# Starting the four folds of the samples' sums later and spacing them closer, with a shorter lead before each add

## The reference, cut to what matters

```python
def block(xb):                       # peer_ffn: tokens by D = 1024
    ...                              # scores, top-16 per head -> eidx, gate
    u = u_tab[eidx]
    a = jax.nn.gelu(jnp.einsum('pd,ped->pe', xb, u))
    coef = gate.astype(xb.dtype) * a
    return jnp.einsum('pe,ped->pd', coef, v_tab[eidx])
...
f = peer_ffn(h, w_q, sub_keys, u_tab, v_tab)
x = x + gt2[:, None, :] * rms_norm(f, g_post2)
```

## Time and profile before

| | |
|---|---|
| median of 3 runs | 1856.24 us (1853.55 to 1856.55) |
| the profiled execution | 1853.55 us, span 1851.7 us |
| mean granted clock of TensorE | 0.982 |
| PE busy over the span | 1769.9 us, 96% |
| DVE busy | 1087.3 us, 59% |
| ACT busy | 584.0 us, 32% |
| POOL busy | 1037.7 us, 56% |
| bytes moved by DMA | 383.61 MB, 207 GB/s on average |

### The profile page before, as it was taken

One profiled execution on the slowest core, in us unless ns is written; L12 is line 12 of the kernel. 1 busy time (PEld: TensorE's weight loads), 2 busy tenths in 40 slices (PEclk: granted clock), 3 DMA queues, 4 the chain that ended last, 5 costly groups with the idle time before them and its releaser, 6 DMA issues.

```text
span 1851.7 us, 31249 instructions
## 1 busy us (share of the span) xinstructions
PE 1769.9 (96%) x12760; PEld 1710.6 (92%) x12760; DVE 1087.3 (59%) x2181; ACT 584.0 (32%) x753; POOL 1037.7 (56%) x684
## 2 busy tenths in 40 slices
PE   5799998899999999999999999999999999999996
PEld 4799975778999999999999999999999999999995
DVE  4731464545747746666664222222788889888884
ACT  5313151333323332233232222222333333333332
POOL 0240010000577778888888888773776777767630
PEclk9899997899999999999999999999999999999998
DMA  7332275766346666575666766666999999999971
GB/s 270 128 146 78 95 290 204 228 202 223 88 87 129 140 129 138 104 155 121 138 124 133 150 138 138 138 138 206 350 374 364 379 366 373 358 372 373 373 299 47
DMA packets 191399, 383.61 MB, mean 207 GB/s; under 512 B 74192, under 2 KB 131920, under 8 KB 176280
## 3 DMA queue, kind: packets, MB, share of 16 engines
q1 hardware_dynamic: 111576, 307.08, 49.3%
q0 software_dynamic: 79680, 74.53, 18.5%
HBM read 316.86 MB, written 64.18 MB: 206 GB/s over the span
## 4 chain that ended last, share of the span: by engine, by line
PE 56%; DVE 9%; issue 5%; DMA 1%; ACT 0%; DVEq 0%; SPq 0%; ACTq 0%
PE ps L1474 29%; PE ps L1454 27%; DVE ul L1644 2%; DVE topi L134 1%; DVE topi L124 1%; DMA ahead_dram<-a 1%; DVE top L128 1%; PE ps L1431 0%; DVE h L227 0%; DVE h L222 0%; DVE h L213 0%; DVE pick L217 0%; DVE pick L234 0%; DVE h L206 0%; ACT uh L1511 0%
## 5 line engine op out<-in xcount | busy, mean ns | idle before, releaser
L99 POOL DMA_INDIRECT gates_dram<-gate,where x384 | 642.6, 1674 | 331.1 <-DVE where L250 187.1
L1454 PE MATMUL ps<-hl,uh 128*128 128x260 f32 x2048 | 414.2, 283 | 8.8 <-DVE ul L1644 8.8
L1454 PE MATMUL ps<-hh,ul 128*128 128x260 f32 x2048 | 413.9, 284 | 0.0
L1454 PE MATMUL ps<-hh,uh 128*128 128x260 f32 x2048 | 413.3, 283 | 0.0
L1644 DVE TENSOR_TENSOR ul<-us,uh 128x1024 fp32r<-128x1024 f32 x132 | 161.2, 1224 | 363.8 <-issue 276.0
L1474 PE MATMUL ps<-cl,uh 128*128 128x384 f32 (+1 forms) x1024 | 344.7, 337 | 0.7 <-issue 0.7
L1474 PE MATMUL ps<-ch,uh 128*128 128x384 f32 x1024 | 344.1, 336 | 0.0
L1474 PE MATMUL ps<-ch,ul 128*128 128x384 f32 x1024 | 344.1, 336 | 0.0
L1454 PEld LDWEIGHTS ps<-hl,uh 128*128 128x128 f32 x2048 | 316.9, 189 | 9.9 <-DVE ul L1644 9.7
L1454 PEld LDWEIGHTS ps<-hh,ul 128*128 128x128 f32 x2048 | 316.9, 189 | 0.0
L1454 PEld LDWEIGHTS ps<-hh,uh 128*128 128x128 f32 x2048 | 316.1, 189 | 0.0
(11 more groups left out here) (212 smaller groups left out, 2233.8 us busy)
## 6 DMA issues: line engine op xcount, KB each, us to landing
us<-utab SPq DMA_DIRECT2D x128, 512.0 KB
pairs<-vtab SPq DMA_DIRECT2D x62, 1024.0 KB
wr<-w_ada SPq DMA_DIRECT2D x24, 1024.0 KB, 6.2
gates_dram<-blank SPq DMA_DIRECT2D x24, 1024.0 KB, 8.6
ahead_dram<-a SPq DMA_DIRECT2D x128, 192.0 KB
qp<-ahead_dram SPq DMA_DIRECT2D x32, 768.0 KB
gt<-gates_dram SPq DMA_DIRECT2D x32, 768.0 KB
wr<-w_in SPq DMA_DIRECT2D x14, 1024.0 KB, 4.8
```

The source lines that it names most:

```text
L99: nc.gpsimd.indirect_dma_start(out=io["gates"].rearrange("g p c a t -> (g p c a t)").unsqueeze(1), out_offset=bass.IndirectOffsetOnAxis(ap ...
L1454: last = nc.tensor.matmul(out[:, half, :], w, r[:, k, half * TH:(half + 1) * TH], start=(k == 0 and q == 0), stop=(k == KD - 1 and q == 2))
```

## The change

The first copy moves from step 24 to step 30, the spacing from 10 steps to 4, and the add from 7 steps behind its copy to `FOLD_EVERY // 2` = 2 steps behind it. `SAMPLES_AT`, which is derived, moves from 64 to 46, and with it the root on ACT and `sample_norm`. No instruction and no transfer is added or taken out.

| | SP's copies | DVE's adds | sample_sums | root | sample_norm |
|---|---|---|---|---|---|
| before, steps | 24, 34, 44, 54 | 31, 41, 51, 61 | 64 | 66 | 68 |
| after, steps | 30, 34, 38, 42 | 32, 36, 40, 44 | 46 | 48 | 50 |

```diff
@@ -1215,7 +1215,7 @@
     PACK_AT, PACKED_AT = 84, 88
     FOLDS = (64, 32, 16, 8)
-    FOLD_AT, FOLD_EVERY, FOLD_LAG = 24, 10, 7
+    FOLD_AT, FOLD_EVERY = 30, 4
     SAMPLES_AT = FOLD_AT + FOLD_EVERY * len(FOLDS)
@@ -1744,7 +1744,7 @@
                     while n >= 0 and sums[0] < summed(n):
                         gathered()
-                    fold_n, at = divmod(n - FOLD_AT - FOLD_LAG, FOLD_EVERY)
+                    fold_n, at = divmod(n - FOLD_AT - FOLD_EVERY // 2, FOLD_EVERY)
                     if at == 0 and 0 <= fold_n < len(FOLDS):
                         fold(fold_n)
```

## The result

The changed kernel takes 1867.56 us (median of 5 runs, 1863.71 to 1873.51), the kernel before 1856.24 (5 runs, 1853.35 to 1857.68). The ratio is 1.0059 [1.0036, 1.0084]: slower by 0.59%, some 11.0 us (0.0059 x 1856). The ratio is formed from the undisturbed executions and need not be the quotient of two medians. I predicted 4.75 us and a time of 1861.0, at most 1866.5. The sign was right. The size was not: the loss is more than twice the sum, and the time lies 1.1 us above the range.

What follows compares the result with a forecast made beforehand. PE was taken to bound the second loop. Its waits of 0.2 + 0.5 + 2.05 + 1.15 + 0.85 sum to 4.75 us, added to the median 1856.24 for 1861.0 us, range 1855.5 to 1866.5.

Steps and rivals of the forecast that it cites:

- The work fits: Steps 32 to 50: DVE's moved work, 8.0 us plus double gathers 4.2 and small products 0.6, against 16.9 us recoverable.
- The account of DVE's lateness: Second loop: DVE's lateness per step falls 0.89 us, grows by added work; PE waits for any excess over 4.4 us.
- L: Time from a fold copy's issue to its landing: between 7.2 and 11.2 us, taken as 10.3, with 0.6 more for fold 0.
- with 10.9 the first adds 2.65: Fold 0, issued at step 30: a copy landing after 10.9 us adds 2.65 us to DVE's lateness.
- D(33): DVE's lateness at the start of step 33, behind fold 0's add: 3.45 us, with no loss of PE.
- what waits behind DVE's stalled add: Claimed `ul`, `cl` and next coefficients, hence PE; SP's loads up to 4 us late but with lead; POOL's gather merely following its buffer.
- 4.4 us of lead: Second loop at rest: DVE has `ul` ready 4.4 us early, so PE waits only when DVE is later than that.
- L1694 where they didn't: Sign in DVE's gather waits: new waits there would mean the queue is slower under the new order than assumed.
- The clock: PE's waits in the loop, up to 2.05 us, counted as causing no lower clock; one such stretch would add about 1.7 us.
- the longer loss: Rival, chance 0.13: bursts in full queues hold a copy or gather longer; landing after 12 us loses 11.5 us, 1866 to 1870.
- The copies in time: Rival, chance 0.32: copies land in under about 9 us, DVE never exceeds its lead, time 1856.2 to 1858 us.
- The faster kernel: Rival, chance 0.03: steps 51 to 68 lose 5.75 us of DVE's work; time 1856.2 us or immeasurably under it.

Runs made afterwards that it cites:

- the gap: DVE waits in every loop step for its own coefficient product (L1673) to end; on the changed kernel 1861.79 us, on the kernel before 1855.47 us.
- experiments 8: The changed kernel with the add 3 steps behind its copy instead of 2, and the gap in every step: 1856.22 us, 1.0002.
- experiment 10: The changed kernel with the gap, and SP issuing the copy ahead of the loads `aa` and `gt` of the same step: 1854.74 us, 0.9988.
- experiment 5: The changed kernel with the gap in every step, copies still issued by SP behind the loads: 1861.79 us, 1.0034 against the kernel before.
- experiment 2: The changed kernel with the add 3 steps behind its copy instead of 2, without the gap: 1865.3 us, 1.0035 against the kernel before.
- experiment 4: The changed kernel with SP copying only 64 of the 1024 columns, without the gap: 1864.12 us, 1.0059 against the kernel before.
- experiment 12: The kernel before with one more 400-element DVE add in steps 20 to 119, and the gap in every step: 1873.09 us, 1.0089.

## Why the prediction was half right

**The bound, the place and the sign were right.** PE bounds the loop; PE's waits in it all stand at L1474, behind `ul`. `sample_sums` costs PE 0.53 us (predicted 0.85). The work fits, as I had added it up: with copies in time and the gap, the 19 steps lose nothing (experiments 8 and 10, both with a loop of 536.8 us).

**The account of DVE's lateness was right for fold 0, its L was not.** The term "with 10.9 the first adds 2.65" was mis-sized: L was 14.0 us in the changed kernel, 12.5 in experiment 5 (1431.82 - 1419.27). With 14.0 the account gives D(33) = 0.8 + 14.0 - 8.25 = 6.55, thus a wait of PE of 2.15 us; measured 2.41. With the 12.5 of experiment 5 it gives 0.7; measured 1.00. These are its only sharp tests. The trace before had the number: its copy of fold 0 passed its last packet 13.5 us after the issue. I had read 9 to 10 us from the mean packet size of one stretch, where half of its rows were through and not the last. For the others I took 10.3; before, their last packets ended after 9.8, 9.7 and 8.0 us, so the value was fair there. In experiment 5 the adds of folds 1 and 2 began 10.2 and 8.8 us after the issue. In the changed kernel fold 2's add took 9.2, and folds 1 and 3 were through after 5.5 and 7.0 us. So L was too short for fold 0 and too long for the rest. I predicted waits at the adds of 1.8, 3.4, 3.6 and 2.0 us, and the changed kernel had 4.95, 0, 1.64 and 0. Why the copies take so long is only in part known. For fold 1 a sixteenth of the bytes changes nothing (10.5 us), so what stands ahead matters; in ACT's queue, with nothing ahead, the last packets came 1.3 to 3.7 us sooner, but fold 0's still after 8.0; ahead of the loads they came 1 us sooner at most (experiment 10). The place in the queue is thus part of it and not all. The 2.0 us plus bytes of the Trainium skill, "DMA: Bandwidth & Descriptors", Anatomy of one DMA, gave an estimate of 2.6 us for the copy. This case's trace doesn't agree with that as a time under load: even alone in ACT's queue fold 0's add began 9.2 to 9.4 us after the issue.

**The step that failed** is the last part of "what waits behind DVE's stalled add": "and POOL's next gather, which only follows the use of its buffer". I costed the gathers at nothing. They do follow the use of their buffer, but the time that their issue takes also depends on DVE's pauses. At rest DVE pauses 0.8 us in each step. A late DVE skips that pause. I had put this down as pure gain (0.89 us won back a step), and it is just this state in which an issue can take 4 to 15.5 us. Then DVE runs out of gathers: it waited 3.98 us in the changed kernel, and up to 7.80 in experiment 2. With what it was late already, that is more than its 4.4 us of lead. That is the wait "L1694 where they didn't", which I had named as a sign of a slower queue; the transfers weren't slower, the issues were. The kernel before already holds two, 4.09 us at 1428.38 and 5.70 at 1505.37, the second as a fold's add ended, the first 5 us behind one. At the second, DVE is late behind the add of fold 2 and skips its next pauses, and POOL's issue beside it lasts until 1511.07, 0.8 us after the next pause began (1510.75 - 0.51 = 1510.24):

```profile
1504.10 1.27 DVE L1701 TENSOR_TENSOR fg<-fg,keys 16x1024 f32<-16x1024 f32 x1
...
1510.75 0.56 DVE L1678 TENSOR_TENSOR cl<-qp,ch 128x384 fp32r<-128x384 f32 x1 [0.51 <-ACT ch L1540]
```

```profile
1505.37 5.70 POOL L1608 DMA_INDIRECT qp<-vtab,packed_choice  x1 [0.30 <-issue]
```

There a single add made DVE late, it was back at its pauses after two steps, and the 4.4 us covered the rest.

**How much is whose.** Removing the held issues alone takes the loss from 11.0 to 6.3 us. Making the copies punctual alone leaves +6.5 with a third step, where no add waits. With small copies (+10.9) and in ACT's queue (+12.8) one or two adds still waited, up to 2.4 us. With the gap as well these are +0.4, +1.7 and +1.1 us. With the third step the two savings, 4.7 and 4.5 us, nearly add up to the 10.6 of both, within their intervals; with the other two they don't, since sooner copies alone saved nothing. That a late copy takes away DVE's pauses, and a held gather makes DVE later still, would explain this; it is argued. With held gathers gone, 6.3 us remain (4.5 to 8.2 by its interval), for late copies. The profiled execution of that kernel is 8.0 us longer than before: 2.8 of them ahead of the loop, 0.8 behind it, where the kernels do not differ, and 4.5 in the loop. That is close to the 4.75 predicted for late copies alone, but in part by luck, for it does not lie where it was predicted. PE's matmuls waited 1.00 us behind fold 0 (predicted: nothing), 0.95 and 0.35 behind fold 1 (0.7), 0.37 behind fold 2 (2.05), nothing behind fold 3 (1.15) and 0.36 behind `sample_sums` (0.85).

**The clock.** "My waits are up to 2.05 us, so I count none, but one such stretch would add about 1.7 us": the stretch came, at the end of a wait of 2.41 us, and cost about that. In the loops of all profiled executions every wait of PE of 2.56 us or more has such a stretch beside it, none of 1.65 us or less has, and of the four between, 2.41 (twice), 2.34 and 2.23, one of 2.41 hasn't (experiment 4). The stretch of experiment 2, at its wait of 5.77 us:

```profile
1478.50:1485.30 6.80, 4.76 (x15) 4.76 (x16) 6.80 (x9) 1.47 (x2) 5.47 (x5) 0.50 0.76 260
```

**The rivals.** Of the longer loss I had the outcome (1866 to 1870; 1867.56 came) and named a held gather in passing, from the 2.57 us in the earlier trace rows, but priced it by L = 12, hence as a transfer held in its queue. It got 0.13. The row that should have raised it was in the trace: the issue of 5.70 us at 1505.37, among 136 with a median of 1.3, in the very loop and just behind a fold's add, with that wait of 2.57 at 1519.24 after it. The copies in time fell with fold 0's 14.0 us. The faster kernel did not come: the 5.75 us of work taken from steps 51 to 68 bought nothing, as PE was never short there.

## What to carry over

An engine that stands idle for a moment in each step may be giving another engine its only chance to get work out: before counting that pause as slack that can be used up, look at the longest, not the median, duration of what the neighbour issues. Where long issues show up, try a deliberate short wait in the busy engine's step; here under 0.1 us of pause in each step was worth 5 to 12 us. It cost nothing in the kernel before, and gained nothing where DVE's work was itself near the bound (experiment 12). And a DMA's lead is read from the last of its packets in a trace of the loaded kernel, not from the mean of its packets: for the 256 KB of fold 0 the last one ended 10.5 to 13.5 us after the issue in SP's queue behind the loads (nine executions), and 8.0 to 8.4 in ACT's own queue (two).

## What the hardware showed that I had not expected

The issue of an indirect gather of 128 rows by POOL takes 0.94 to 1.3 us as a rule. In the seven kernels without the gap (one execution each) 19 issues took over 4 us, up to 15.5, all beside a DVE that ran one instruction behind the other. Fourteen of them ended 0.76 to 0.83 us after DVE's next pause began, however short: four of these pauses lasted only 0.04 to 0.06 us. Four ended during `sample_sums`, 0.9 us after the start of its first product, where the trace shows no pause; that product reads the same tile as both its inputs. One, in experiment 2, ended 0.28 us after a pause began. In the seven kernels with the gap, 0.12 us more from start to start in each step, none of the 272 issues of each was over 2.15 us.

The Trainium skill, "SBUF — State Buffer", Who interferes with whom, says that a DVE instruction with two SBUF inputs contends with a GpSimd instruction that reads SBUF; the same page's table, Summary: rules for kernel authors, adds that the second to issue is fully blocked until the first finishes. The trace agrees in kind: DVE's instructions of this loop have two or more inputs in SBUF, and the gather reads its list of rows, `packed_choice`, from there. It does not agree with that section's report of a probe in which `tensor_tensor` did not stall DMA: here issues were held beside it. Nor does it agree in size: the hold outlasted a single instruction many times over (15.5 us, where the longest of DVE's instructions takes 1.3). That these ports are the cause is argued, not shown; the holds that ended inside a product of one tile with itself would fit it, but a DVE whose instructions have one SBUF input was not tried. Why only a few issues are held, while most pass beside a busy DVE in 1.3 us, stays open too. Twelve of the 19 began during one of the 28 adds of the folds or as it ended, and 13 of the 19 within 0.04 us of the end of some DVE instruction. So something in how the two instructions meet may matter besides the pauses; no run here separates it.
